# Samples' inter-chunk numerators: the states streamed past 32-column slices of queries, then picked by columns of the identity

## The reference, cut to what matters

```python
# mLSTM
num = jnp.einsum('btsh,bshv->bthv', qk, vc) + w_inter[..., None] * jnp.einsum('bthk,bhkv->bthv', qc, C)
...
# GLA
o = jnp.einsum('btsh,bshv->bthv', att, vc) + jnp.einsum('bthk,bhkv->bthv', qc * jnp.exp(b), S)
```

## Time and profile before

| | before |
|---|---|
| median of three runs | 2382.94 us (2374.94 to 2383.36) |
| the profiled execution, its own time | 2379.16 us |
| its span, first to last instruction | 2377.4 us |
| TensorE busy | 2340.4 us, 98% |
| VectorE busy | 1079.6 us, 45% |
| ScalarE busy | 666.0 us, 28% |
| mean granted TensorE clock | 0.989 of full |

### The profile page before, as it was taken

The page is one execution under the profiler, slowest core; times in us unless marked ns, Lnnn a source line. Parts: engine busy times, 40 slices in busy tenths (PEclk is TensorE's granted clock), DMA queues, the critical chain, the costliest instruction groups (busy, mean ns, idle before and its releaser), DMA issues.

```text
span 2377.4 us, 39495 instructions
## 1 busy us (share of the span) xinstructions
PE 2340.4 (98%) x17304; PEld 2308.7 (97%) x17304; DVE 1079.6 (45%) x1395; ACT 666.0 (28%) x806; POOL 29.7 (1%) x20
## 2 busy tenths in 40 slices
PE   7999999999999999999999999999999999999997
PEld 7999999999999999999999999999989899999997
DVE  5334334684545433324553343353754454334245
ACT  4212222453423222212332121244221332122122
POOL 0000000000000000000000000000000100000000
PEclk9999999999989999999999999999998999999999
DMA  4222222232322222222322222222122222222221
GB/s 173 88 89 71 89 79 63 89 115 88 112 88 79 89 88 72 88 89 62 98 80 81 88 73 86 80 80 89 54 74 74 93 72 88 89 81 79 89 68 61
DMA packets 72552, 201.29 MB, mean 85 GB/s; under 512 B 7268, under 2 KB 26980, under 8 KB 72448
## 3 DMA queue, kind: packets, MB, share of 16 engines
q1 hardware_dynamic: 72448, 199.80, 26.0%
HBM read 187.82 MB, written 11.95 MB: 84 GB/s over the span
## 4 chain that ended last, share of the span: by engine, by line
PE 91%; DVE 4%; issue 3%; ACT 1%; POOL 0%; DMA 0%; DVEq 0%; SPq 0%; POOLq 0%; ACTq 0%
PE ps L436 82%; PE ps L646 3%; PE ps L531 1%; PE ps L516 1%; PE ps L688 1%; DVE w_lo L1472 1%; PE ps L666 1%; DVE og L1639 0%; PE ps L677 0%; PE ps L695 0%; PE ps L680 0%; PE ps L535 0%; DVE x L2123 0%; PE ps L487 0%; POOL scratch L1452 0%
## 5 line engine op out<-in xcount | busy, mean ns | idle before, releaser
L436 PE MATMUL ps<-xn_hi,w_hi 128*128 128x288 f32 x3328 | 721.2, 298 | 12.8 <-DVE w_lo L1472 11.5
L436 PE MATMUL ps<-xn_hi,w_lo 128*128 128x288 f32 x3328 | 714.3, 296 | 0.0
L436 PE MATMUL ps<-xn_lo,w_hi 128*128 128x288 f32 x3328 | 714.1, 296 | 0.0
L436 PEld LDWEIGHTS ps<-xn_hi,w_hi 128*128 128x128 f32 x3328 | 537.4, 189 | 17.4 <-DVE w_lo L1472 11.5
L436 PEld LDWEIGHTS ps<-xn_hi,w_lo 128*128 128x128 f32 x3328 | 537.9, 189 | 0.0
L436 PEld LDWEIGHTS ps<-xn_lo,w_hi 128*128 128x128 f32 x3328 | 537.8, 189 | 0.0
L1074 ACT ACTIVATE w_hi<-raw 128x1024 fp32r<-128x1024 f32 x332 | 331.3, 1046 | 361.3 <-PE ps L436 327.4
L1472 DVE TENSOR_TENSOR w_lo<-raw,w_hi 128x1024 fp32r<-128x1024 f32 x332 | 393.4, 1226 | 40.4 <-ACT w_hi L1074 38.3
L436 PE MATMUL ps<-h_lo,w_hi 128*128 128x288 f32 x1616 | 352.2, 297 | 2.6 <-DVE h_hi L1785 2.6
L436 PE MATMUL ps<-h_hi,w_hi 128*128 128x288 f32 x1616 | 352.0, 297 | 1.4 <-DVE w_lo L1472 1.4
L1517 DVE TENSOR_TENSOR scratch<-ps,rstd 128x576 f32<-128x576 f32 x88 | 66.7, 758 | 537.0 <-PE ps L436 533.9
(11 more groups left out here) (229 smaller groups left out, 1590.8 us busy)
## 6 DMA issues: line engine op xcount, KB each, us to landing
raw<-in_w_gate SPq DMA_DIRECT2D x88, 512.0 KB, 3.3
raw<-in_w_up SPq DMA_DIRECT2D x88, 512.0 KB, 4.4
raw<-in_w_down SPq DMA_DIRECT2D x64, 512.0 KB, 3.7
raw<-in_w_mix SPq DMA_DIRECT2D x64, 512.0 KB, 4.2
raw<-in_w_down SPq DMA_DIRECT2D x32, 384.0 KB, 3.7
state_s<-in_state_c SPq DMA_DIRECT2D x4, 1024.0 KB, 7.1
out_c_s<-state_s SPq DMA_DIRECT2D x4, 1024.0 KB, 4.5
state_s<-in_state_g SPq DMA_DIRECT2D x4, 1024.0 KB, 6.7
```

Of the source, the lines that this page charges most:

```text
L436: ins = nc.tensor.matmul(o, a, b[:, c] if c is not None else b, start=first and j == 0, stop=last and j == 2)
```

## The change

`sample_piece` is replaced by three functions. At the first call (i = 0) `sample_stage` runs four float32 matmuls, one for each pair of samples: the stationary operand is a slice of 32 query columns that begins with the pair's 16, the moving one is the two samples' states (512 columns). Matmul j writes PSUM partitions 32j to 32j + 31, so that the four stand in four column groups of the array. ScalarE copies the whole bank to SBUF (`take_stage`, 128 x 512). At the last call `sample_numerator` waits for that copy, and for each half runs the old product from 64 partitions first and then two matmuls that take the copied rows as the stationary operand and 32 chosen columns of the identity as the moving one; these pick each sample's own rows and transpose them, added to the same PSUM region. The calls between do nothing. The copy goes to `T(4)` in the mLSTM mixer and to a new tile `late_stage` in GLA, which lies over the convolution's small tiles.

```diff
+        def staged(mixer):
+            return late_stage[:, :, :] if mixer else T(4)[:, 0:2 * DV].rearrange("p (i n) -> p i n", n=DV)
...
-            def sample_piece(mixer, h, bank, i, n):
-                a, per = 2 * i // n, 2 * DEC_BATCH // n
-                vs = slice(h * DV + a * P, h * DV + (a + 1) * P)
-                ds = slice(a * P, (a + 1) * P)
-                first = (i % (n // 2)) * per
-                for b in range(first, first + per):
-                    ts = slice(b * DEC_SEQ, (b + 1) * DEC_SEQ)
-                    nc.tensor.matmul(ps[:, bank, a * SAMPLE + b * DEC_SEQ:a * SAMPLE + (b + 1) * DEC_SEQ],
-                                     state_s[:, b, ds], qt[:, h, ts],
-                                     start=b == 0, stop=True, skip_group_check=True)
-                if first + per == DEC_BATCH:
-                    ins = nc.tensor.matmul(ps[:, bank, a * SAMPLE:(a + 1) * SAMPLE], v_tok[0:SAMPLE, 0, vs],
-                                           att(mixer, h)[0:SAMPLE, SEQ:TOK], start=False, stop=True,
-                                           skip_group_check=True)
-                    if a == 1 and mixer == 1:
-                        ins.then_inc(num_s_done, 1)
+            def sample_stage(mixer, h, bank):
+                for j in range(4):
+                    ins = nc.tensor.matmul(ps[32 * j:32 * (j + 1), bank, :], qt[:, h, 16 * j:16 * j + 32],
+                                           state_s[:, 2 * j:2 * j + 2, :], start=True, stop=True)
+                ins.then_inc(stage_done, 1)
+
+            def sample_numerator(mixer, h, bank):
+                pe.wait_ge(stage_taken, N_HEADS * mixer + h + 1)
+                for a in range(2):
+                    vs = slice(h * DV + a * P, h * DV + (a + 1) * P)
+                    out = ps[:, bank, a * SAMPLE:(a + 1) * SAMPLE]
+                    nc.tensor.matmul(out, v_tok[0:SAMPLE, 0, vs], att(mixer, h)[0:SAMPLE, SEQ:TOK],
+                                     start=True, stop=True, skip_group_check=True)
+                    for i in range(2):
+                        ins = nc.tensor.matmul(out.rearrange("p (j r) -> p j r", r=16)[:, :, 8 * i:8 * i + 8],
+                                               staged(mixer)[:, i, a * P:(a + 1) * P],
+                                               ident.rearrange("p (j r) -> p j r", r=32)[:, :, 8 * i:8 * i + 8],
+                                               start=False, stop=True, skip_group_check=True)
+                if mixer == 1:
+                    ins.then_inc(num_s_done, 1)
+
+            def sample_pieces(mixer, h, bank):
+                def at(i, n):
+                    if i == 0:
+                        sample_stage(mixer, h, bank)
+                    elif i == n - 1:
+                        sample_numerator(mixer, h, bank)
+                return at
...
+            def take_stage(mixer, h, bank):
+                u = N_HEADS * mixer + h
+                act.wait_ge(stage_done, u + 1)
+                nc.scalar.activation(staged(mixer), ps[:, bank, :].rearrange("p (i n) -> p i n", n=DV), ACT.Copy)\
+                    .then_inc(stage_taken, 1)
```

More of the change, by code:

```diff
@@ L134, in program @@
         level_mask = sb("level_mask", [P, len(LEVELS) + 1, P], mybir.dt.uint8)
-        conv_w = sb("conv_w", [P, KT_X, CONV_W + 1])
-        conv_in = sb("conv_in", [P, KT_X, DEC_BATCH, TAIL])
-        conv_out = sb("conv_out", [P, KT_X, DEC_BATCH + 1, TAIL])
+        conv_w = inner.enter_context(nc.sbuf_tensor("conv_w", [P, KT_X, CONV_W + 1], f32))
+        conv_in = inner.enter_context(nc.sbuf_tensor("conv_in", [P, KT_X, DEC_BATCH, TAIL], f32))
+        conv_out = inner.enter_context(nc.sbuf_tensor("conv_out", [P, KT_X, DEC_BATCH + 1, TAIL], f32))
+        inner.close()
+        late_stage = sb("late_stage", [P, 2, DV])
         gate_raw = v_tok[:, 1, 0:G_ALL]
@@ L276, in program @@
         keys_b_done, hsq_sum = sem("keys_b_done"), sem("hsq_sum")
+        stage_done, stage_taken = sem("stage_done"), sem("stage_taken")
         num_s_done, ht_s_ready, hsq_s_done, us_half, st_half = (sem(n) for n in (
@@ L757, in sample_part @@
                     pe.wait_ge(state_in, 16 * (h + 1))
-                    return lambda i, n: sample_piece(0, h, 7, i, n)
+                    return sample_pieces(0, h, 7)
                 def sample_den(h):
@@ L886, in sample_part @@
                         pe.wait_ge(hvar_ready, N_HEADS + h)
-                    return lambda i, n: sample_piece(1, h, bank, i, n)
+                    return sample_pieces(1, h, bank)
                 def sample_updates_of(h, part, bank):
@@ L1268, in mlstm_mix @@
                 for h in range(1, N_HEADS):
+                    if h > 1:
+                        take_stage(0, h - 1, 7)
                     second_gate(h - 1)
@@ L1275, in mlstm_mix @@
                         split_at(3)
+                        take_stage(0, 0, 7)
                         den_size(0)
@@ L1286, in mlstm_mix @@
                         exponentials(h + 1)
+                take_stage(0, 3, 7)
                 second_gate(3)
@@ L1349, in gla_mix @@
                     gate_block(1, 2 * h + 2, mx_free, MX_O[1][h + 1])
+                    take_stage(1, h, 4)
                     sample_squares(1, h, 4)
@@ L1357, in gla_mix @@
                 split_at(7)
+                take_stage(1, 2, 7)
                 sample_squares(1, 2, 7)
@@ L1363, in gla_mix @@
                 gate_block(1, 6, mx_free, MX_O[1][3])
+                take_stage(1, 3, 7)
                 gate_block(1, 7, psum_free, base + O_AT[1][3] + 1)
```

## The result

The changed kernel takes 2356.96 us, the median of four runs (2355.60 to 2362.78), against 2383.15 (2374.94 to 2393.25): ratio 0.9907, 95% interval 0.9881 to 0.9933 (the ratios here are estimates with their intervals, not quotients of the two medians, which would be 0.9890). The forecast was 2372, range 2358 to 2390; the median lies 1 us under the range and 15 under the forecast. The direction was right, the size was not.

The account below looks back on a forecast made before the run. TensorE, busy 98% of the span, was taken to bound the kernel. From the profiled 2379.2 us, +1.3 for the units' work (4.44 against 4.28 us each) and -8.6 for the clock gave 2372 us, range 2358 to 2390.

Parts of the forecast that it names:

- What bounds the kernel: Whole kernel: TensorE, busy 98% of the span, bounds it; its time counts one for one.
- Numerators: Last call of a unit: two halves, each one product at 0.36 and picks at 0.36 and 0.20, together 1.84 us.
- The way out of a GLA unit: Change from the last pick into f32r work: 0.10 us, entered in the sum as 0.12 for every unit.
- Stage: Four float32 matmuls at a unit's first call: 2.15 us streaming plus 0.33 for changes, 2.48 us.
- five slots: Stage's eight records start in strict order, a group's second waiting for its first: 5 x 0.43 = 2.15 us.
- case 3: Stage: all four column groups run at once, 0.86 us, a unit 3.15, kernel 2362 us; chance 0.12.
- The wait: Numerators wait for ScalarE's 0.60 us copy; f32r work covers it, cost nothing; without cover 0.6 a unit.
- The clock: Around the eight units: of 15.3 us lost at 1.2 GHz, 6.7 stays (1.7 at each mLSTM unit), so -8.6 us.
- The sum: Whole kernel: profiled 2379.2 + 1.3 for the work - 8.6 for the clock = 2372 us.
- case 4: Stage: the column groups don't overlap, 3.44 us, kernel 2382 us; chance 0.18.
- Case 5: Numerators as one dense thin run: clock falls in more units, 5.1 us in all eight, kernel 2406 us; chance 0.10.
- Case 2: Clock around the units: the loss stays near 15 us, stage as forecast, kernel 2380 us; chance 0.18.

Follow-up runs that it names:

- halves: The changed kernel with each stage matmul cut into two of 256 columns, neighbours in the same column group: 2358.52 us, ratio 0.9901.
- full_width: The changed kernel with each stage matmul loading 128 query columns and writing all 128 PSUM partitions, so no column groups: 2375.61 us, ratio 0.9975.
- no_cover: The changed kernel with the stage moved to the last call, right before the numerators, so no f32r work covers ScalarE's copy: 2373.02 us, ratio 0.9967.
- after_again: The changed kernel unaltered, run once more on one chip beside the second run of grouped: 2357.01 us, ratio 0.9896.
- grouped: The changed kernel with products from 64 partitions together (mLSTM denominator's included), then the four picks: 2352.31 us, ratio 0.9876; run again 2351.00 us.
- thin_back: The changed kernel with each pick run four times, so a unit ends in 16 small matmuls: 2397.58 us, ratio 1.0080.

## Why the prediction missed by 15 us

- **What bounds the kernel**: right. TensorE's busy time and the span shrank together, by 22.3 and 22.5 us.
- **Numerators**: right, 1.84 forecast, 1.84 in the chain, and the 0.14 into the denominator too. The way out of a GLA unit was wrong by a little: the sum added 0.12 for it after the change and counted none before, but work behind line 535 paid 0.11 more than work behind a pick. With it the eight units gain 10.0 us where the forecast's terms, with the stage as measured, give 9.1.
- **Stage**: this step failed. It put the streaming at 2.15, five slots, "with starts in order"; it took two, 0.86. The changes were sized rightly (0.33 put, 0.13 + 0.19 measured), so the slots alone are 1.3 us a unit, 10.3 of the 15. The premise that a neighbour's first record must wait for a group's second one is false: four first records start together, and halves shows that even four records of one group, in a row in the program, don't hold up the others. That is case 3, to which I gave 0.12, with a sum of 3.15 for a unit; measured 3.02 + 0.14 = 3.16 at mLSTM head 1. The Trainium skill's span (TensorE: Matmul & The Clock Gate, Part 3: Packing small matmuls) would have given this: two slots of 0.43. Full width takes 3.43, so the gain is 3.5 times for four groups. I weighed an argument of mine, which no row supported, above it.
- **The wait**: right, at nothing; the copy had 0.7 us to spare at mLSTM head 0 and 1.9 at head 1. Its price without cover, 0.6, measured 0.58. In no_cover the clock adds more than twice that, from the wait or from the stage's new place.
- **The clock**: right mechanism, size short. Forecast -8.6; measured -11.9 at the units and -1.7 behind idle time elsewhere. I kept 1.7 for each of four mLSTM units; two fell. These two begin just behind line 786, in the mLSTM mixer where I put them. That it was two is partly chance: after_again has two as well, at heads 1 and 3, and grouped, with 0.5 us less there, has none.
- **The sum** with measured terms: 2379.2 - 10.0 - 13.5 = 2355.7; the profiled execution took 2356.68. The 1.0 between them is not explained.
- **The other cases**: case 4, no overlap, was built as full_width: 2375.6, forecast 2382. Case 5's mechanism, a dense run of thin work that brings falls, exists: thin_back shows it with 16 picks in a unit. With four picks behind 18 f32r matmuls it hardly acts; with four picks right behind the stage and the wait (no_cover) the clock fell at seven units. Case 2, a loss that stays, did not come.

## What to carry to other kernels

Small matmuls had two prices here: the weight load each, and a clock that may fall to 1.2 GHz though TensorE never idles. Before reshaping them, read the granted clock in windows of some us around them; streaming more columns behind each load can pay even when the columns are of no use. Independent products of at most 32 output rows with long moving operands can be put in the four column groups, and the result picked out of a copy later; do products from 64 partitions together, apart from those from 128, and leave other dense work between the stage and whoever waits for its copy.

## What the runs showed that I had not expected

- Four float32 matmuls of 512 columns in four column groups take 0.99 us, one alone on the full array 0.86, four there 3.43. Their eight weight loads of 32 columns, about 108 ns each, overlap and are done in 0.16 us.
- Streaming 128 instead of 8 columns in 128 matmuls made the kernel before some 16 us faster, for some 1.4 us more work (7.65 for 7.48 in a unit), with the clock at 0.997 for 0.989.
- The Trainium skill (TensorE: Matmul & The Clock Gate, "Why this matters for your kernels") names idle gaps between bursts of matmuls as what lowers the clock. Here the falls around idle time cost the kernel before 5.0 us, and the thin work, with TensorE busy all the time, 15.3.
